# The last five weight tiles of a decoder trunk, each brought by two transfers of unequal numbers of partitions

## The reference, cut to what matters

```python
q = (xb @ w_q).reshape(P_BLOCK, P_HEADS, P_QDIM)
s1 = einsum('thd,nd->thn', q[..., :P_HALF], k1)
s2 = einsum('thd,nd->thn', q[..., P_HALF:], k2)
...                                     # 16 best of the sums of both: eid, gate
u_e = jnp.take(u_tab, eid, axis=0)      # (128, 8, 16, 1024)
act = gelu(einsum('thkd,td->thk', u_e, xb))
v_e = jnp.take(v_tab, eid, axis=0)
return einsum('thk,thkd->td', gate * act, v_e)
```

## Time and profile before

| | us |
|---|---|
| median of 3 runs | 1525.19 (1523.71 to 1525.28) |
| the profiled execution's own time | 1525.57 |
| its span, first to last instruction | 1523.8 |
| PE busy | 1353.0 |
| DVE busy | 1050.6 |
| ACT busy | 656.6 |
| POOL busy | 598.0 |
| moved by DMA | 619.26 MB, mean 406 GB/s |

### The profile page before, as it was taken

The page is one execution under the profiler, slowest core; times in us unless marked ns, Lnnn a source line. Parts: engine busy times, 40 slices in busy tenths (PEclk is TensorE's granted clock), DMA queues, the critical chain, the costliest instruction groups (busy, mean ns, idle before and its releaser), DMA issues.

```text
span 1523.8 us, 15431 instructions
## 1 busy us (share of the span) xinstructions
PE 1353.0 (89%) x4376; PEld 723.6 (47%) x4376; DVE 1050.6 (69%) x2684; ACT 656.6 (43%) x1728; POOL 598.0 (39%) x542
## 2 busy tenths in 40 slices
PE   9999987889787899989988999999998889887776
PEld 7886544445442464444343655445444345432322
DVE  5588677777667768767676665777776766666765
ACT  5665333333233555544433544655343433333333
POOL 0101344454455433435444323434444344444442
PEclk9999999999999999999999999999999999999999
DMA  7886999999999999999999999999999999999997
GB/s 261 296 344 246 425 426 426 427 427 427 426 426 424 420 425 426 426 418 425 427 425 417 423 426 426 401 426 408 426 426 425 427 427 426 427 425 426 426 408 289
DMA packets 96837, 619.26 MB, mean 406 GB/s; under 512 B 10970, under 2 KB 11114, under 8 KB 31216
## 3 DMA queue, kind: packets, MB, share of 16 engines
q0 software_dynamic: 75584, 542.70, 85.2%
q1 hardware_dynamic: 21024, 75.32, 12.7%
q10 hardware_dynamic: 144, 0.26, 0.0%
HBM read 617.19 MB, written 1.05 MB: 406 GB/s over the span
## 4 chain that ended last, share of the span: by engine, by line
PE 43%; DMA 33%; DVE 16%; issue 4%; ACT 2%; POOL 1%; ACTq 0%; POOLq 0%; SPq 0%; DVEq 0%
PE psum L1481 42%; DMA row<-in_uv,ids 32%; DVE row L1238 7%; ACT gate_diag L779 1%; POOL row L569 1%; ACT diag L789 1%; DMA row<-in_uv,half_ids 1%; DVE look L1166 1%; DVE numbers L1171 1%; DVE topi L1105 0%; DVE scores L1097 0%; DVE topi L1094 0%; DVE tile_lo L939 0%; DVE look L1169 0%; DMA x<-in_x 0%
## 5 line engine op out<-in xcount | busy, mean ns | idle before, releaser
L1481 PE MATMUL psum<-row,diag 128*128 128x512 f32 x1976 | 939.7, 618 | 154.3 <-ACT diag L789 151.9
L569 POOL DMA_INDIRECT row<-in_uv,ids x508 | 577.9, 1138 | 827.1 <-PE psum L1481 716.0
L1238 DVE SCALAR_TENSOR_TENSOR row<-row,hn 128x1024 f32<-128x1024 f32 x512 | 623.3, 1224 | 387.7 <-DMA row<-in_uv,ids 373.9
L1481 PEld LDWEIGHTS psum<-row,diag 128*128 128x128 f32 x1976 | 370.1, 196 | 628.7 <-issue 378.8
L769 ACT ACTIVATE acted<-dots 128x2 f32<-128x2 f32 x256 | 52.2, 204 | 718.9 <-DVE row L1238 711.3
L789 ACT ACTIVATE diag<-gate_diag,acted 128x128 f32<-128x128 f32 x496 | 174.5, 387 | 0.1
L779 ACT ACTIVATE gate_diag<-ident,gate 128x128 f32<-128x128 f32 x496 | 169.0, 386 | 1.2 <-DVE gate L1230 0.8
L939 DVE TENSOR_TENSOR tile_lo<-raw,tile_hi 128x1024 fp32r<-128x1024 f32 x32 | 39.7, 1240 | 28.0 <-ACT tile_hi L615 27.8
L1481 PEld LDWEIGHTS psum<-hT_query,raw 128*128 128x128 f32 x416 | 50.3, 192 | 11.0 <-issue 11.0
L1481 PE MATMUL psum<-hT_query,raw 128*128 128x128 f32 x416 | 50.6, 275 | 0.0
L615 ACT ACTIVATE tile_hi<-raw 128x1024 fp32r<-128x1024 f32 x32 | 33.9, 1060 | 34.6 <-PE psum L1481 34.4
(11 more groups left out here) (261 smaller groups left out, 1150.5 us busy)
## 6 DMA issues: line engine op xcount, KB each, us to landing
raw<-in_a_in SPq DMA_DIRECT2D x32, 512.0 KB, 4.3
raw<-in_w_q SPq DMA_DIRECT2D x28, 512.0 KB, 16.7
raw<-in_b_rv SPq DMA_DIRECT2D x19, 512.0 KB
row<-in_uv,ids POOLq DMA_INDIRECT x508
raw<-in_b_qk SPq DMA_DIRECT2D x14, 512.0 KB
aout<-in_a_out SPq DMA_DIRECT2D x13, 512.0 KB, 8.4
early_q<-in_w_q SPq DMA_DIRECT2D x12, 512.0 KB
kept<-in_a_out SPq DMA_DIRECT2D x3, 512.0 KB, 14.4
```

Source lines behind the costliest of these rows:

```text
L569: pool.indirect_dma_start(rows[s][:, :], None, t[f"uv{l}"][:, :], bass.IndirectOffsetOnAxis(ids[:, n // TOPK % IDS_GROUPS, k:k + 1], 0)).t ...
L1238: dve.scalar_tensor_tensor(u, u, 1.0, hn[:, h, :], ALU.mult, ALU.mult, accum_out=dots[:, n // TOPK % 2, k:k + 1]).then_inc(dotted, 1)
L1481: return pe.matmul(o, a, b, start=start, stop=stop, skip_group_check=True)
```

## The change

The transfers of tiles 53 to 57 are each cut in two along the partitions: the first brings partitions 0 to 119 (126, 117, 108, 100 for the further tiles), the second the rest, 8 (2, 11, 20, 28) partitions. Both go into the same buffer and both increment the same semaphore by 16, so `weight_turn` counts transfers in place of tiles. The second is issued right behind the first, without a wait of its own. Bytes, buffers and PE's work are as before.

```diff
+TILE_PARTS = {len(WEIGHTS) - 5 + i: (first, P - first) for i, first in enumerate((120, 126, 117, 108, 100))}
...
 def weight_turn(m):
-    return 16 * ((N_AIN + RAW_Q) // RAW_SLOTS + m // RING + 1)
+    transfers = sum(len(TILE_PARTS.get(i, (P,))) for i in range(m % RING, m + 1, RING))
+    return 16 * ((N_AIN + RAW_Q) // RAW_SLOTS + transfers)
...
                     sp.wait_ge(weight_used, m - RING + 1)
-                load(t[name][c], m % RING)
+                first = 0
+                for many in TILE_PARTS.get(m, (P,)):
+                    sp.dma_start(raw[m % RING][first:first + many, :], t[name][c][first:first + many]).then_inc(raw_loaded[m % RING], 16)
+                    first += many
```

## The result

| | median, us | lowest to highest | executions |
|---|---|---|---|
| before | 1525.24 | 1523.71 to 1526.84 | 4 |
| changed | 1536.17 | 1535.43 to 1536.94 | 4 |

A forecast was written before the change was run, and what follows sets the result against it. The prediction took DMA bytes at 426 GB/s as the bound, with one late engine setting the end. From the profiled 1525.57 us it took 4.2, giving 1521.4, then 0.38 to the median: 1521.0 us, range 1520.0 to 1527.1.

The forecast's parts named there:

- Bytes set the pace: From about 100 us on, full DMA engines bound the kernel: 1 MB per row at 426 GB/s is 2.46 us.
- Five more issues on SP cost nothing: On SP, five issues of 0.33 us are covered because SP waits for tiles long before they are needed; counted as nothing.
- The tiles were in time as well: At PE's use of the five tiles, some 10 of 28 us are used; late-tile rival: 1528 us or more, chance 0.02.
- Equal shares: Supposition for the divided loads: each transfer is dealt equally, so 120 rows use 15 engines and 126 use 14.
- Always from the same place: Supposition: each transfer's shares begin at the same engine, giving 52 rows on places 0 and 1, 0 on place 15.
- The bytes are the same, so what can change is which engine brings them: For the five tiles, only the sharing among engines shifts, each 4 KB row still costing 0.155 us.
- dealing evenly: Rival: rows of the divided transfers go to all engines anyway, 40 each, so 1525.2 us; chance 0.05.
- One engine is late and sets the end: At the end one of sixteen engines works alone for 3.5 us; at 1505 us it is 6.2 us behind the others' mean.
- It is at place 14 or 15: Main case: the late engine, among the last in dealing order, is relieved and the kernel gains 4.2 us; chance 0.60.
- the ten that get more: Places 0 to 9, loaded 1.6 to 1.9 us more; rival: the late engine is there, 1526.9 us, chance 0.21.
- The length of the lone stretch: Sign at the end: one engine's time alone shrinks from 3.5 us to about nothing if right, grows to some 5 if harmed.
- From the last landing to the end nothing changes: Behind the last landing, PE's products and DVE's line 1264 move along at the same distance to the end.

The follow-up runs named there:

- e1_columns: Kernel before, with the same five tiles each brought by two transfers of all 128 partitions and half the columns: 1525.33 us, 1.0004.
- e15_one_tile: Kernel before, with only the first of the five tiles (tile 53) divided, by 120 and 8 partitions: 1527.3 us, 1.0013.
- e12_extra_5: Kernel before plus 30 HBM-to-HBM transfers of 5 rows of 4 KB after the last tile, loading places 0 to 4: 1529.84 us, 1.0026.
- e5_rates: Separate program without the computation: SP loads 16 tiles by various partition splits, alone or beside POOL's stream; alone 397 GB/s whole, 234 for 64/64.
- e9_rates_sides: Separate program without the computation: divided tiles into SBUF (128, 64/64: 405, 232 GB/s) and from HBM to HBM (315, 307).
- e13_which_64: Separate program without the computation: 64 rows of each tile into different partition ranges; beside POOL's stream 250 GB/s at 0 to 63, 410 at 32 to 95.
- e4_120_8: Kernel before, with the five tiles all divided into transfers of 120 and 8 partitions: 1535.39 us, 1.0066.
- e2_64_64: Kernel before, with the five tiles each divided into two transfers of 64 partitions: 1533.94 us, 1.0061.

## Why the prediction was wrong

**Bytes set the pace: right.** 4658 KB lacking at 427 GB/s make 10.9 us, as much as the loss; no engine's busy time changed by more than the 3.2 us of PE.

**Five more issues on SP cost nothing: right**, by `e1_columns` (1.0004). The tiles were in time as well. PE's waits from 1230 to 1340 us in the changed kernel, largest of PE itself:

```profile
PE psum L1486 <- ACT diag L794: 19.1, 7, 6.0
```

There is none for a transfer into `raw`.

**Equal shares: right**, by the 29 completion packets. **Always from the same place: borne out**, by the step between 3 and 5 rows. Which engines these are, no run shows, since the trace doesn't number them.

**"The bytes are the same, so what can change is which engine brings them", at 0.155 us a row: wrong, and the step that failed.** I took the time of a row of 4 KB to be a property of the engine. The row that I had it from the earlier trace rows is one engine working alone, and the full stream had nothing in it but transfers on all 128 partitions; both give a sixteenth of 426 GB/s. In a divided tile rows take 0.22 us, and the gathers' packets beside them 0.44 in place of 0.31. To which partitions a transfer writes matters: with shares, sizes and number held, it is 250 GB/s for 0 to 63 and 410 for 32 to 95. None of the rivals had this in it. It costs some 2 us for a tile (`e15_one_tile`), 8 to 11 for five. Nor does dealing evenly help, for which a rival had forecast no change: 64/64, with equal shares, made the kernel 8.6 us slower.

**One engine is late and sets the end: right.** Work added on its place costs about what it takes, 4.1 to 5.4 us for 4.65, on the first three places nothing.

**It is at place 14 or 15, chance 0.60: wrong.** It is at 3 or 4. "Duties are handed to the ends of a row" was no reading of the trace, as the text says itself, and no run shows it; a count of places would have given 0.62 to the ten that get more. Even without the slow packets the change would have been a loss, 51 rows in place of 40 on this engine, 1.7 us by the forecast's own sum. In the changed kernel this part doesn't stand apart, since the lacking bytes alone make the loss; what it adds was not shown. The length of the lone stretch, which I had named as the sign, doesn't tell it: in `e12_extra_5` the late engine had 4.65 us more to do and the end came 4.1 us later, and yet one engine worked alone for 3.5 us again (1517.0 to 1520.5 us, share 0.07), because the others finished later as well.

**From the last landing to the end nothing changes: right**, 1.11 and 0.70 us behind it, and 10.04 us of transfer as before.

No run beats the kernel before. To relieve places 3 and 4 a transfer would need to leave them out, and by the step above transfers with fewer shares begin at place 0; this wasn't tried further. Open are why this engine is late, whether it is 3 or 4, and why packets take longer to some ranges of partitions than to others.

## What to carry to other kernels

Where the DMA engines are full, read their share and the rate together: a share of 1.0 at less than the rate of the quiet stretches (here 1.02 at 335 to 343 GB/s, where it was 427) means that packets take longer, and then the cause can be a small transfer on another queue. Load a tile over all 128 partitions and divide it by columns if it must be divided (1.0004 here); the divisions of all five tiles by partitions tried here slowed the gathers that ran at the same time and cost 5.8 to 10.9 us, and equal parts were hardly better than unequal ones (8.6 us for 64/64, 7.8 for 112/16, 10.1 for 120/8). Before work is shifted between DMA engines, find the late one by adding a little work to the first r places and looking where the time steps up (here by 4.1 us from three places to five), with each r on the same chip.

## What the runs showed of the hardware

- Whole tiles of 512 KB ran at 397 to 405 GB/s alone, divided 64/64 at 232 to 234, with all 16 engines busy (share 1.02) (`e5_rates`, `e9_rates_sides`, `e13_which_64`). With a stream of whole transfers beside them both together moved 415 and 305 (`e5_rates`).
- Transfers to 64 partitions ran slowly at 0 to 63, 64 to 127 and 16 to 79 (209, 205 and 211 GB/s), and fast at 32 to 95 (321 alone with a share of 0.88; with a stream beside them 410 in all, against 250 at 0 to 63) (`e13_which_64`).
- A slow transfer on one queue lengthened packets of another: 8 KB of the gathers from 0.31 to 0.44 us (the changed kernel, 1238 to 1248 us).
- One of 16 engines, at place 3 or 4, had at least some 4 us more to do by the end of this kernel than each of the first three (no loss with work added at places 0 to 2, 0.9997, and 4.1 us with 0 to 4).
- The counts of completion packets fit that a transfer from SP into SBUF uses the largest number of engines up to 16 that divides its partitions: for five divided tiles 35 more than for whole ones with 120/8 (`e4_120_8`), 80 with 64/64 (`e2_64_64`), 29 in the changed kernel; for all 16 tiles of `e5_rates` 368 with 120/8, 384 with 100/28.
